# Mixer B's scan: the stabiliser rows arrive by broadcast transfers, and GpSimd makes the mask

## The chip, the cores and the metric

The kernel runs on one core of a Trainium2 chip. The metric is the device time of one execution in microseconds (us). A core has five engines that run on their own and meet at semaphores: TensorE (in the rows PE, its weight loads PEld), VectorE (DVE), ScalarE (ACT), GpSimd (POOL) and SyncE (SP), which here only issues transfers. 16 DMA engines move the data of all transfers.

## The reference

One step of a two-layer backbone with 128 context tokens ("prompt") and 1024 latent tokens, width 1024. Each layer computes modulation vectors from a conditioning vector, mixes tokens in three head groups (A: attention, B: a matrix memory scanned in both directions, C: neighbourhood attention), projects, and runs a channel MLP. The part that matters here is mixer B, 4 heads of 64, which the reference computes in chunks:

```python
def step(carry, xs):
    C, n, m = carry
    ...
    b = jnp.cumsum(fc, axis=1).transpose(0, 2, 1)
    d = jnp.where(causal, b[..., :, None] - b[..., None, :] + ig[..., None, :], -jnp.inf)
    inter = b + m[..., None]
    m_t = jnp.maximum(inter, jnp.max(d, axis=-1))
    w = jnp.einsum('blhd,bshd->bhls', qc, kc) * jnp.exp(d - m_t[..., None])
    w_inter = jnp.exp(inter - m_t)
    num = (jnp.einsum('bhls,bshd->blhd', w, vc)
           + jnp.einsum('bhl,blhk,bhkd->blhd', w_inter, qc, C))
    den = jnp.maximum(jnp.abs(den), jnp.exp(-m_t))
    ...

def modulation(cond, w_ada, b_ada):
    return jnp.split(jax.nn.silu(cond) @ w_ada + b_ada, N_MOD, axis=-1)
```

The running stabiliser m_t enters the weights of a chunk as a row: one value per head and query token, the same for all key tokens. Keys lie on the partitions, so this row has to be present on all 128 of them.

## The kernel before

Each layer runs its sections one after the other with a barrier between them: projection, mixer A, mixer C, mixer B, and the tail (output projection and MLP). The change lies in mixer B (`mixer_b`, lines 1734 to 1983), in what mixer C preloads for it, and in the constants.

**Items.** The scan has 18 items per layer: chunk of 128 tokens and direction, first the prompt's two, then the latent chunks, forward and backward in turn. Item i works on four heads at once. Every engine runs the items in order:

- TensorE, step i: scores(i+1) (line 1774, four products of 128x128, written to PSUM bank 0 or 1), spread(i+1) (line 1779), the product of queries and state (1793), the modulation pieces that belong to the step (430, 438, 447), W(i) (1798, weights times values), U(i) (1804, scaled keys times values).
- spread: four products of a constant selecting matrix `neg_select` with `m_rows`, where the stabiliser's rows of four heads lie on four partitions. The result, minus m_t on all partitions, is in bank 2.
- VectorE: weight(i) (1912, scores times E4), mask(i+1) (1905, spread plus the causal table, into E4), then finish(i-1): the N4 add (1919), four state updates (1926), the normalising steps (1930 to 1934), and for late items a sum of squares (1940).
- ScalarE: exp of E4 (1836), scaling of the state product (1843), and copies for the modulation.
- GpSimd, step i: KS(i), the scaling of the keys (1884), which U(i) needs. Once both directions of a chunk exist it also takes, at step i, the norm of item i-3 (1871, 1872, 1878) and the adding of the two directions of item i-2 (1860, 1864, 1866). Apart from the prompt's, these begin with step 12 (adding) and step 13 (norm), because the two directions meet in the middle.

E4, the exponents, has two buffers: mask(i) waits for weight(i-2).

**The modulation woven in.** The same loop multiplies the conditioning vector with 48 pieces of `w_ada` in layer 0 and 32 in layer 1, 512 KB each, 8 to a vector. They pass through a ring of 6 slots (`mods.w`, in `ring_flat`): piece c is loaded when piece c-6 has been used. Pieces 0 to 2 come from mixer C. Step 1 uses pieces 3 to 5, step 2 pieces 6 and 7, step 6 pieces 16 to 18, step 8 pieces 22 and 23, step 9 none (it turns a row into columns), step 10 pieces 24 to 27, step 11 pieces 28 to 31. SyncE issues all loads in one order; its waits are in that order too. After piece 5 it loads small rows (`load_rows`, which waits for `clear_rows` on GpSimd), and after pieces 17 and 25 it stores a gate row to DRAM, waits for the landing and broadcasts it back to all partitions (`spread_gate`, lines 487 and 491, two loads of 512 KB).

Of the kernel before, what the change touches and what calls it, by code (L numbers as in the profile page):

```python
# [19 lines left out]
ALU = mybir.AluOpType  # L20
# [5 lines left out]
P = 128  # L26
# [63 lines left out]
def shape_constants():  # L90
# [19 lines left out]
    neg_select = np.zeros((P, 2, 4, P), f)  # L110
# [4 lines left out]
    for j in range(4):  # L115
        for d in range(2):
            neg_select[32 * d + j, d, j] = -1
            for t in range(NT):
                r, c = 64 * d + 4 * t + j, LAT - 1 - t if d and t != PROMPT else t
                position[r, c] = 1  # L120
                gather[r, 32 * d + j] = 1
                spread[32 * d + j, r] = 1
                place[r, j, c] = 1
    bias_select = np.zeros((P, 4, 32), f)
    for j in range(4):
# [3 lines left out]
        "outside": np.where(neighbourhood_tables()[1], 0, NEG).astype(f), "neg_select": neg_select,  # L129
# [16 lines left out]
def build(nc, I, O):  # L146
    sems = {}
    with ExitStack() as ctx:
# [60 lines left out]
        neg_select = sb("neg_select_sb", [P, 2, 4, P])  # L209
# [32 lines left out]
        m_rows = rows_at_lo2[:, TABLE:TABLE + TOK]  # L242
# [73 lines left out]
        with nc.Block() as block:  # L316
            @block.sync
            def _(sp):
                for k, t in (("ident", ident[:, :]), ("causal", causal[:, :, :]), ("neg_select", neg_select[:, :, :, :]),
                             ("chunk_tables", chunk_tables[:, :]),  # L320
                             ("bias_select", bias_select[:, :, :])):
                    sp.dma_start(t, I[k]).then_inc(sem("constants_loaded"), 16)
                sp.wait_ge(sem("constants_loaded"), 5 * 16)
# [22 lines left out]
        for l in range(DEPTH):  # L346
# [18 lines left out]
            C_LOADS, C_TABLE_LOADS = 12 * 16, 2 * 16  # L365

# [1291 lines left out]
            def mixer_c():  # L1658
                with ExitStack() as own:
# [23 lines left out]
                    with nc.Block() as block:  # L1683
# [5 lines left out]
                        def _(pool):  # L1689
                            clear_low(pool, c_sets[1][2])  # L1690
                            pool.sem_inc(sem("c_low_cleared"), 1)
                            pool_step(pool.memset(m_rows, 0.0))
                            pool.sem_inc(sem("m_rows_cleared"), 1)
# [12 lines left out]
                        def _(sp):  # L1706
                            load_c(sp, 1, sem("c_loaded1"), sem("c_tables_loaded1"))
                            sp.wait_ge(sem("m_rows_cleared"), 1)
                            for d in range(2):
                                sp.dma_start(m_rows[32 * d:32 * d + 4, :].rearrange("h (t s) -> h t s", s=P),  # L1710
                                             stabiliser_dram[d].rearrange("t h s -> h t s")).then_inc(sem("b_loaded"), 16)
# [22 lines left out]
            def mixer_b():  # L1734
                with ExitStack() as own:
# [29 lines left out]
                    with nc.Block() as block:  # L1765
                        @block.tensor
                        def _(pe):
                            def scores(i):
                                d, t, c = work[i]
                                tt = slice(t * P, (t + 1) * P)  # L1770
                                if i >= 2:
                                    pe.wait_ge(sem("b_weighted"), i - 1)
                                for h in range(4):
                                    mm = pe.matmul(ps[:, i % 2, h * P:(h + 1) * P], kT[:, h // 2, h % 2, tt], qT[:, h // 2, tt], start=True, stop=True)
                                mm.then_inc(sem("b_scores"), 1)
                                if i >= 1:
                                    pe.wait_ge(sem("b_masked"), i)
                                for h in range(4):
                                    mm = pe.matmul(ps[:, 2, h * P:(h + 1) * P], neg_select[:, d, h, :], m_rows[:, tt], start=True, stop=True)
                                mm.then_inc(sem("b_stabiliser_spread"), 1)  # L1780
# [73 lines left out]
                        def _(pool):  # L1854
# [24 lines left out]

                            mods.clear_rows(pool)  # L1880
                            for i, (d, t, c) in enumerate(work):
                                if i >= 2:
                                    pool.wait_ge(sem("b_updated"), i - 1)
# [15 lines left out]
                        def _(dve):  # L1899
                            def mask(i):  # L1900
                                d, t, c = work[i]
                                dve.wait_ge(sem("b_stabiliser_spread"), i + 1)
                                if i >= 2:
                                    dve.wait_ge(sem("b_weighted"), i - 1)
                                dve.tensor_tensor(E4[:, i % 2, :].rearrange("p (h t) -> p h t", h=4), ps[:, 2, :].rearrange("p (h t) -> p h t", h=4),
                                                  causal[:, d:d + 1, :].to_broadcast([P, 4, P]), ALU.add).then_inc(sem("b_masked"), 1)

                            def weight(i):
                                dve.wait_ge(sem("b_exp"), i + 1)
                                if i >= 2:  # L1910
                                    dve.wait_ge(sem("b_applied"), i - 1)
# [30 lines left out]
                            mask(0)  # L1942
                            for i in range(nw):
                                weight(i)
                                if i + 1 < nw:
                                    mask(i + 1)
# [20 lines left out]
                        def _(sp):  # L1967
                            for c in range(3, mods.n * KD):
                                mods.load(sp, c)
                                if c == 5:  # L1970
                                    mods.load_rows(sp)
                                if c in (17, 25):
                                    mods.spread_gate(sp, mods.gates[c // 25])
# [522 lines left out]
```

## Time and profile before

| | us |
|---|---|
| median of 3 runs (lowest, highest) | 3462.75 (3461.22, 3467.98) |
| the profiled execution | 3457.57 |
| its span, first to last instruction | 3455.6 |
| TensorE busy in it | 3221.2 (93%) |
| VectorE, ScalarE, GpSimd busy | 1335.3, 1526.0, 1515.8 |
| share of the 16 DMA engines' time that the queues' packets took | 39.8% |
| mixer B's scan, layer 0 | 687.3 to 796 |
| mixer B's scan, layer 1 | 2392.2 to 2499 |

The span is what lies between the first and the last instruction; the execution's time has about 2 us around it. Times in the rows count from the span's start. A row of the timeline gives start and length of a run of equal instructions, with the idle time of the engine before it in square brackets and what ended that. A fp32 product of 128x128 shows as two instructions.

### The profile page before, as it was taken

How to read it: one execution, taken by the hardware profiler on the slowest of the kernel's cores; microseconds unless marked ns; L12 is line 12 of the kernel's file. 1: busy time of each engine (PE TensorE's matmuls, PEld its weight loads, DVE VectorE, ACT ScalarE, POOL GpSimd, SP SyncE). 2: the span in 40 equal slices, each digit the busy share in tenths (PEclk: the TensorE clock that was granted, in tenths of full speed). 3: DMA queues.
4: the chain of work that ended last, by engine and by line, in shares of the span. 5: the costliest groups of instructions: out<-in, count | busy, mean ns of one | idle time of the engine just before them, and what ended most of it. 6: DMA issues, size and time to landing. Idle time of an engine off the chain costs nothing. (4 is left out here: it accounts for less than half of the span.)

```text
span 3455.6 us, 50657 instructions
## 1 busy us (share of the span) xinstructions
PE 3221.2 (93%) x19786; PEld 2869.0 (83%) x19786; DVE 1335.3 (39%) x2283; ACT 1526.0 (44%) x2904; POOL 1515.8 (44%) x880
## 2 busy tenths in 40 slices
PE   4999899897899999999979998998789999999998
PEld 2999787785789889989869996887677899999897
DVE  3154366675621141141123435666756113112112
ACT  4223355544554454454442234554356444444443
POOL 1352101136655565565544321011467556556554
PEclk6999899998999999999989998999899999999999
DMA  5222401674544444444431223036355445444443
GB/s 202 55 81 99 127 1 43 176 278 135 174 130 125 145 134 126 143 133 124 145 101 41 85 102 110 1 90 200 131 175 160 127 125 162 128 124 153 139 123 115
DMA packets 357948, 429.43 MB, mean 124 GB/s; under 512 B 35328, under 2 KB 290320, under 8 KB 357200
## 3 DMA queue, kind: packets, MB, share of 16 engines
q1 hardware_dynamic: 357568, 426.07, 39.8%
q8 instruction: 159, 2.61, 0.3%
q14 instruction: 77, 0.63, 0.1%
q10 hardware_dynamic: 144, 0.13, 0.0%
HBM read 375.56 MB, written 50.57 MB: 123 GB/s over the span
## 5 line engine op out<-in xcount | busy, mean ns | idle before, releaser
L2330 POOL TENSOR_TENSOR w_lo<-w_raw,w_hi 128x1024 fp32r<-128x1024 f32 x432 | 1053.3, 2439 | 730.6 <-ACT w_hi L2251 730.5
L2251 ACT CAST w_hi<-w_raw 128x1024 fp32r<-128x1024 f32 x432 | 453.2, 1049 | 921.7 <-PE ps L2201 548.8
L2360 DVE TENSOR_TENSOR u_lo<-mix,u_hi 128x384 fp32r<-128x384 f32 x192 | 265.2, 1381 | 1208.0 <-ACT u_hi L2262 1208.0
L2199 PE MATMUL ps<-h_hi,w_hi 128*128 128x384 f32 x1536 | 519.8, 338 | 2.5 <-ACT mix L2258 2.5
L2201 PE MATMUL ps<-h_hi,w_lo 128*128 128x384 f32 x1536 | 519.1, 338 | 0.0
L2200 PE MATMUL ps<-h_lo,w_hi 128*128 128x384 f32 x1536 | 518.3, 337 | 0.0
L2216 PE MATMUL ps<-w_hi,u_hi 128*128 128x512 f32 x1152 | 456.1, 396 | 0.0
L2218 PE MATMUL ps<-w_hi,u_lo 128*128 128x512 f32 x1152 | 455.5, 395 | 0.0
L2217 PE MATMUL ps<-w_lo,u_hi 128*128 128x512 f32 x1152 | 454.6, 395 | 0.0
L1185 PE MATMUL ps<-h_hi,p_w_hi 128*128 128x384 f32 x960 | 331.0, 345 | 21.7 <-POOL p_w_lo L1399 21.7
L1187 PE MATMUL ps<-h_hi,p_w_lo 128*128 128x384 f32 x960 | 324.3, 338 | 0.0
L1186 PE MATMUL ps<-h_lo,p_w_hi 128*128 128x384 f32 x960 | 324.3, 338 | 0.0
L2199 PEld LDWEIGHTS ps<-h_hi,w_hi 128*128 128x128 f32 x1536 | 290.0, 189 | 11.0 <-issue 2.9
L2200 PEld LDWEIGHTS ps<-h_lo,w_hi 128*128 128x128 f32 x1536 | 290.0, 189 | 8.3
L2201 PEld LDWEIGHTS ps<-h_hi,w_lo 128*128 128x128 f32 x1536 | 289.9, 189 | 0.0
L2218 PEld LDWEIGHTS ps<-w_hi,u_lo 128*128 128x128 f32 x1152 | 216.3, 188 | 52.1
L2217 PEld LDWEIGHTS ps<-w_lo,u_hi 128*128 128x128 f32 x1152 | 216.6, 188 | 43.5
L2216 PEld LDWEIGHTS ps<-w_hi,u_hi 128*128 128x128 f32 x1152 | 216.7, 188 | 43.3
L1399 POOL TENSOR_TENSOR p_w_lo<-w_raw,p_w_hi 128x1024 fp32r<-128x1024 f32 x40 | 95.9, 2399 | 351.7 <-ACT p_w_hi L1294 351.7
L1185 PEld LDWEIGHTS ps<-h_hi,p_w_hi 128*128 128x128 f32 x960 | 181.9, 189 | 22.9 <-POOL p_w_lo L1399 22.5
L770 DVE TENSOR_REDUCE small<-ps 128x1 f32<-128x1152 f32 (+1 forms) x108 | 133.9, 1239 | 140.2 <-PE ps L688 139.9
L1186 PEld LDWEIGHTS ps<-h_lo,p_w_hi 128*128 128x128 f32 x960 | 182.0, 190 | 0.0
(267 smaller groups left out, 5294.8 us busy)
## 6 DMA issues: line engine op xcount, KB each, us to landing
w_raw<-in_w_ffn_up SPq DMA_DIRECT2D x192, 512.0 KB, 4.0
w_raw<-in_w_ffn_down SPq DMA_DIRECT2D x192, 512.0 KB, 3.3
ring<-in_w_ada SPq DMA_DIRECT2D x80, 512.0 KB, 5.9
w_raw<-in_w_in SPq DMA_DIRECT2D x34, 512.0 KB, 4.0
out_y_sample<-x SPq DMA_DIRECT2D x32, 512.0 KB, 3.0
w_raw<-in_w_out SPq DMA_DIRECT2D x30, 512.0 KB, 3.5
x<-out_y_sample SPq DMA_DIRECT2D x24, 512.0 KB, 4.9
w_raw<-in_w_out SPq DMA_DIRECT2D x36, 256.0 KB, 4.2
```

The source lines that it names most:

```text
L1185: pe.matmul(bank(q, CW), wh[:, k, :], hi[:, k, cc], start=(k == 0), stop=False)
L1186: pe.matmul(bank(q, CW), wh[:, k, :], lo(n)[:, k, :], start=False, stop=False)
L1187: mm = pe.matmul(bank(q, CW), wl[:, k, :], hi[:, k, cc], start=False, stop=(k == KD - 1))
L2199: pe.matmul(ps[:, 6, 0:CW], wh[:, k, :], hi[:, k, cc], start=(k == 0), stop=False)
L2200: pe.matmul(ps[:, 6, 0:CW], wh[:, k, :], lo(n)[:, k, :], start=False, stop=False)
L2201: mm = pe.matmul(ps[:, 6, 0:CW], wl[:, k, :], hi[:, k, cc], start=False, stop=(k == KD - 1))
L2216: pe.matmul(ps[:, b, :], a, w_hi[:, s % 3, cc], start=first, stop=False)
L2217: pe.matmul(ps[:, b, :], a, w_lo[:, s % 3, cc], start=False, stop=False)
L2218: mm = pe.matmul(ps[:, b, :], a_lo, w_hi[:, s % 3, cc], start=False, stop=end)
L2251: act.copy(w_hi[:, i % 3, :], raw[:, i % 3, :]).then_inc(sem("piece_hi"), 1)
L2330: pool.tensor_tensor(w_lo[:, i % 3, :], raw[:, i % 3, :], w_hi[:, i % 3, :].bitcast(F32), ALU.subtract).then_inc(sem("piece_lo"), 1)
L2360: dve.tensor_tensor(u_lo[:, j % 2, m, :], square[:, i % 2, :], u_hi[:, j % 2, m, :].bitcast(F32), ALU.subtract).then_inc(sem("m_u_lo"), 1)
```

## The change

The matmuls of the spread and the constant `neg_select` go. Instead the stabiliser rows of an item, 4 heads x 128 values = 2 KB in DRAM, are broadcast by one transfer to all 128 partitions (256 KB written), into one of five buffers. Rows of items 0 and 1 are loaded in mixer C, those of 2 to 4 at the start of the scan ahead of piece 3, that of item i+5 at SyncE's step i, after mask(i) is done. The mask moves from VectorE to GpSimd, is causal table minus row, and no longer reads PSUM. GpSimd makes mask(i+1) at the start of its step i, ahead of KS(i); masks 0 and 1 come ahead of `clear_rows`. weight(i) waits for scores(i) itself. SyncE now loads pieces by the step that frees their slot.

```diff
@@ shape_constants, build @@
-    neg_select = np.zeros((P, 2, 4, P), f)
...
-            neg_select[32 * d + j, d, j] = -1
...
-        m_rows = rows_at_lo2[:, TABLE:TABLE + TOK]
+        STABILISERS = 5
+        stabilisers = [rows_at_lo2[:, a:a + 4 * P] for a in (TABLE, TABLE + 512, TABLE + 1024, 0, 512)]
...
-                for k, t in (("ident", ident[:, :]), ("causal", causal[:, :, :]), ("neg_select", neg_select[:, :, :, :]),
+                for k, t in (("ident", ident[:, :]), ("causal", causal[:, :, :]), 
...
+            def load_stabilisers(sp, i, d, t, loaded):
+
+                row = stabiliser_dram[d, t:t + 1].rearrange("a h s -> a (h s)")
+                sp.dma_start(stabilisers[i % STABILISERS], row.to_broadcast([P, 4 * P])).then_inc(loaded, 16)
@@ mixer_c, GpSimd and SyncE @@
-                            pool_step(pool.memset(m_rows, 0.0))
-                            pool.sem_inc(sem("m_rows_cleared"), 1)
...
-                            sp.wait_ge(sem("m_rows_cleared"), 1)
                             for d in range(2):
-                                sp.dma_start(m_rows[32 * d:32 * d + 4, :].rearrange("h (t s) -> h t s", s=P),
-                                             stabiliser_dram[d].rearrange("t h s -> h t s")).then_inc(sem("b_loaded"), 16)
+                                load_stabilisers(sp, d, d, PROMPT, sem("b_loaded"))
@@ mixer_b, TensorE @@
-                                if i >= 1:
-                                    pe.wait_ge(sem("b_masked"), i)
-                                for h in range(4):
-                                    mm = pe.matmul(ps[:, 2, h * P:(h + 1) * P], neg_select[:, d, h, :], m_rows[:, tt], start=True, stop=True)
-                                mm.then_inc(sem("b_stabiliser_spread"), 1)
@@ mixer_b, GpSimd @@
+                            def mask(i):
+                                d, t, c = work[i]
+                                if i >= 2:
+                                    pool.wait_ge(sem(f"b_stabilisers_loaded{i % STABILISERS}"), 16 * ((i - 2) // STABILISERS + 1 if i % STABILISERS >= 2 else i // STABILISERS))
+                                    pool.wait_ge(sem("b_weighted"), i - 1)
+                                pool.tensor_tensor(E4[:, i % 2, :].rearrange("p (h t) -> p h t", h=4), causal[:, d:d + 1, :].to_broadcast([P, 4, P]),
+                                                   stabilisers[i % STABILISERS].rearrange("p (h t) -> p h t", h=4), ALU.subtract).then_inc(sem("b_masked"), 1)
+
+                            mask(0)
+                            mask(1)
                             mods.clear_rows(pool)
                             for i, (d, t, c) in enumerate(work):
+                                if 2 <= i + 1 < nw:
+                                    mask(i + 1)
@@ mixer_b, VectorE @@
-                            def mask(i):
...
                             def weight(i):
                                 dve.wait_ge(sem("b_exp"), i + 1)
+                                dve.wait_ge(sem("b_scores"), i + 1)
...
-                                if i + 1 < nw:
-                                    mask(i + 1)
@@ mixer_b, SyncE @@
-                            for c in range(3, mods.n * KD):
+                            def load_later(i):
+                                d, t, c = work[i]
+                                if i >= STABILISERS:
+                                    sp.wait_ge(sem("b_masked"), i - STABILISERS + 1)
+                                load_stabilisers(sp, i, d, t, sem(f"b_stabilisers_loaded{i % STABILISERS}"))
+
+                            step_of = {c: i for i in range(nw) for c in mod_pieces(i)}
+                            for i in range(2, STABILISERS):
+                                load_later(i)
+                            for c in range(3, mods.ring):
                                 mods.load(sp, c)
-                                if c == 5:
-                                    mods.load_rows(sp)
-                                if c in (17, 25):
-                                    mods.spread_gate(sp, mods.gates[c // 25])
+                            mods.load_rows(sp)
+                            for i in range(nw):
+                                if i + STABILISERS < nw:
+                                    load_later(i + STABILISERS)
+                                for c in range(mods.ring, mods.n * KD):
+                                    if step_of[c - mods.ring] == i:
+                                        mods.load(sp, c)
+                                        if c in (17, 25):
+                                            mods.spread_gate(sp, mods.gates[c // 25])
```

## Rows read from the trace of the kernel before

**Rows 1.** Timeline of layer 0's scan, TensorE in step 8: start, length, operation

```profile
733.09 0.97 PEld L1774 LDWEIGHTS ps<-hT 128*128 128x128 f32 x8
733.98 0.97 PEld L1779 LDWEIGHTS ps<-rows_at_lo,neg_select_sb 128*128 128x128 f32 x8
734.87 0.53 PEld L1793 LDWEIGHTS ps<-b_first,hT 128*128 128x128 f32 x4
...
736.95 0.97 PEld L1798 LDWEIGHTS ps<-b_first,b_weights 128*128 128x128 f32 x8 [0.41 <-issue]
...
738.29 0.97 PEld L1774 LDWEIGHTS ps<-hT 128*128 128x128 f32 x8
```

**Rows 2.** The same timeline, VectorE's weight(8)

```profile
733.37 0.69 DVE L1912 TENSOR_TENSOR b_weights<-ps,b_exponents 128x512 f32<-128x512 f32 x1 [0.21 <-DVE mix L1934]
```

**Rows 3.** SyncE's own waits, 686 to 790 us: total, times, longest

```profile
SPq L422 <- PE ps L430: 59.2, 20, 9.1
```

**Rows 4.** Windows: busy time by engine, granted clock, DMA share, GB/s

```profile
702.00:705.00 3.00, 3.00 (x36) 2.54 (x38) 1.86 (x5) 0.78 (x4) 0.00 (x0) 1.00 0.99 386
726.00:729.00 3.00, 3.00 (x31) 2.59 (x31) 2.29 (x8) 1.13 (x4) 0.61 (x1) 1.00 1.03 403
747.00:757.00 10.00, 10.00 (x112) 8.43 (x105) 5.72 (x18) 3.16 (x12) 3.29 (x5) 1.00 0.97 350
...
687.00:797.00 110.00, 96.90 (x1016) 81.06 (x1016) 77.73 (x215) 45.05 (x182) 44.91 (x68) 0.95 0.67 237
```

**Rows 5.** Timeline of GpSimd, steps 15 to 16 of layer 0

```profile
770.98 0.67 POOL L1884 TENSOR_TENSOR b_scaled_keys<-b_first,b_columns 128x256 f32<-128x256 f32 x1
771.83 0.19 POOL L1871 TENSOR_SCALAR small<-small 128x4 f32<-128x4 f32 x1 [0.18 <-DVE small L1940]
...
776.20 0.62 POOL L1884 TENSOR_TENSOR b_scaled_keys<-b_first,b_columns 128x256 f32<-128x256 f32 x1
```

**Rows 6.** Groups of GpSimd's instructions by shape, whole span: busy, mean ns

```profile
L1427 POOL TENSOR_TENSOR p_work<-mix,cos_sb 128x512 f32<-128x512 f32 x16 | 23.7, 1481 | 24.9 <-DVE mix L1458 24.9
L1433 POOL TENSOR_TENSOR p_work<-mix 128x512 f32<-128x512 f32 x18 | 21.2, 1182 | 0.0
```

**Rows 7.** Timeline of GpSimd at the scan's start

```profile
687.31 1.38 POOL L399 MEMSET mlp_mods_bias<- 128x1536 f32 x1 [24.52 <-remote]
```

**Rows 8.** Timeline of SyncE's issues in layer 0's scan

```profile
694.41 21.15 SPq L422 DMA_DIRECT2D ring<-in_w_ada  x12
715.60 1.19 SPq L487 DMA_DIRECT2D gate_rows<-mlp_mods_row  x4
718.94 0.82 SPq L491 DMA_DIRECT2D gate<-gate_rows  x2
```

**Rows 9.** Transfers issued 82 to 90 us: count, size, us to landing

```profile
cos_sb<-in_cos SPq DMA_DIRECT2D x1, 256.0 KB, 4.2
```

**Rows 10.** Windows, while the cosine table was in flight

```profile
85.50:86.00 0.50, 0.50 (x3) 0.50 (x3) 0.00 (x0) 0.47 (x1) 0.50 (x1) 0.50 1.18 403
```

**Rows 11.** Windows, while a gate row's two broadcasts were in flight

```profile
738.00:739.00 1.00, 1.00 (x11) 1.00 (x11) 0.68 (x2) 0.64 (x3) 0.36 (x1) 1.00 0.98 246
739.00:740.00 1.00, 1.00 (x12) 1.00 (x11) 0.36 (x1) 0.00 (x0) 0.26 (x1) 1.00 0.98 397
```

**Rows 12.** Timelines of VectorE: weight(12) and N4 of item 17, both layers

```profile
755.13 0.69 DVE L1912 TENSOR_TENSOR b_weights<-ps,b_exponents 128x512 f32<-128x512 f32 x1 [1.18 <-ACT b_exponents L1836]
...
787.34 0.43 DVE L1919 TENSOR_TENSOR b_intra<-ps,b_inter 128x260 f32<-128x260 f32 x1
...
2459.45 0.69 DVE L1912 TENSOR_TENSOR b_weights<-ps,b_exponents 128x512 f32<-128x512 f32 x1 [1.18 <-ACT b_exponents L1836]
...
2490.94 0.43 DVE L1919 TENSOR_TENSOR b_intra<-ps,b_inter 128x260 f32<-128x260 f32 x1
```

**Rows 13.** Timeline of SyncE at the start of the kernel

```profile
1.62 0.43 SPq L322 DMA_DIRECT2D neg_select_sb<-in_neg_select  x1
...
7.21 4.08 SPq L422 DMA_DIRECT2D w_ada_ring<-in_w_ada  x8
```

More of the change, by code:

```diff
@@ L128, in shape_constants @@
         "ident": ident, "cos": cos.copy(), "sin": sin.copy(), "causal": causal,
-        "outside": np.where(neighbourhood_tables()[1], 0, NEG).astype(f), "neg_select": neg_select,
+        "outside": np.where(neighbourhood_tables()[1], 0, NEG).astype(f),
         "chunk_tables": np.concatenate([position, gather, spread, place.reshape(P, 4 * NT)], 1), "bias_select": bias_select,
@@ L208, in build @@
         causal = sb("causal_sb", [P, 2, P])
-        neg_select = sb("neg_select_sb", [P, 2, 4, P])
         chunk_tables = sb("chunk_tables_sb", [P, NT + 36 + P + 4 * NT])
@@ L322, in _ @@
                     sp.dma_start(t, I[k]).then_inc(sem("constants_loaded"), 16)
-                sp.wait_ge(sem("constants_loaded"), 5 * 16)
+                sp.wait_ge(sem("constants_loaded"), 4 * 16)
             @block.gpsimd
@@ L1899, in _ @@
                         def _(dve):
-                            def mask(i):
[L1901 to L1906, printed above, removed]
                             def weight(i):
                                 dve.wait_ge(sem("b_exp"), i + 1)
+                                dve.wait_ge(sem("b_scores"), i + 1)
                                 if i >= 2:
@@ L1940, in sum_squares @@
                                 dve.tensor_reduce(ss[:, t, :], squares[:, n % 2, :].rearrange("p (h d) -> p h d", d=HD), AX.X, ALU.add).then_inc(sem("b_out_summed"), 1)
-                            mask(0)
                             for i in range(nw):
                                 weight(i)
-                                if i + 1 < nw:
-                                    mask(i + 1)
                                 if i >= 1:
```

## The prediction

> **What bounds the kernel now.** I read the page first: TensorE is busy 93% of the span, so time has to come off TensorE, or off a stretch where it waits. Then I read the stretch that the change touches, the scan of mixer B, which runs from 687.3 to 796 us in layer 0 and from 2392.2 to 2499 us in layer 1, on the timeline. One step of the loop is scores(i+1), spread(i+1), the state product, the weight pieces of the modulation, W(i) and U(i). In [rows 1] step 8 starts with its scores at 733.09 and step 9 at 738.29: 5.20 us, with TensorE's weight loads back to back but for 0.41 us, in which the 256-column products of the pieces still run. The spread takes 733.98 to 734.87, that is 0.89 us. VectorE in the same step [rows 2] starts weight(8) at 733.37, 3.6 us before W(8) needs it at 736.95: it isn't the bound. SyncE waits 59.2 us in all until TensorE has used a piece [rows 3]: the ring of pieces follows TensorE now. Reader, see here that TensorE bounds steps 1 to 11 and that the transfers are close behind: a window of 3 us reaches 403 GB/s at a share of 1.03 [rows 4].
>
> From step 13 on GpSimd is full. From one scaling of keys to the next it takes 5.22 us, of which 0.18 us is waiting [rows 5].
>
> **TensorE without the spread.** Steps 1 to 11 lose 11 x 0.89 = 9.8 us. In step 9 (no pieces) TensorE also waited about 0.8 us for VectorE's state update, which sat behind mask(10); with the mask off VectorE that goes too. At the start the first two spreads ran at the low clock; there I take 1.4 us. That is 12.0 us a layer, if nothing else is late. What is late next has to be looked for in the transfers and on GpSimd.
>
> **The transfers up to step 11.** SyncE's queue is in order. It gets three stabiliser loads ahead of pieces 3 to 5. Then it waits until GpSimd has cleared the modulation's rows. GpSimd now first makes mask(0) and mask(1). The nearest row is a 128x512 tensor_tensor with two tensors, one of them broadcast along the middle axis, at 1.48 us (one with a single input tensor took 1.18) [rows 6]; I take 1.48, because the mask also reads two tensors. So the clearing (1.38 us [rows 7] and a second memset of about 0.5) ends at about 692.4 instead of 689.3, and the small loads behind it, which ended just before 694.41 [rows 8], end at about 696.9. Piece 6 is issued there instead of at 694.41.
>
> From then on the queue never runs dry in my sum; this is its load until piece 31, the last one that step 11 needs:
> - pieces 6 to 31, 26 of 512 KB. At share 1 the windows give 386 to 403 GB/s [rows 4]; at 395 GB/s one takes 1.33 us: 34.6 us.
> - stabiliser rows 5 to 15, 11 of 256 KB in packets of 2 KB, none of which the scan has now. The nearest row by size is the cosine table, also 256 KB in rows of 2 KB [rows 9]; while it and its like were in flight the rate was 403 GB/s [rows 10]: 0.65 us. The nearest by kind is the gate row's broadcast, which started at 246 GB/s [rows 11]: 1.07 us, the upper bound. I take 0.70, since in the second half of the gate pair the rate was at 397: 7.7 us.
> - two pairs of gate broadcasts, 3.5 us each: 1.05 MB at about 300 GB/s, between the 246 and the 397 of [rows 11]: 7.0 us.
> - two bubbles. SyncE stores the gate row, waits for its landing and only then issues the broadcasts: 3.34 us from 715.60 to 718.94 [rows 8]. Now the stores stand behind a full queue, so the queue drains while SyncE waits; from landing to first data is 1.1 us, and landing trails the data by about 1.1: 2.2 us each, 4.4 us.
>
> Started at 699.2 (issue at 696.9 plus 2.3), the sum is 699.2 + 34.6 + 7.7 + 7.0 + 4.4 = 752.9. Landing, the last product, the bias, W(11) and U(11) add 3.2: step 12 starts at 756.1. Before it starts 0.38 us ahead of weight(12), which begins at 755.13 [rows 12]: 754.75. So the 12.0 us from the spreads are gone, and 1.3 us more. The reason in one line: three steps carry 8 pieces and now 3 stabiliser rows, 12.7 us of transfer in 12.9 us of shortened steps, and nothing is left for 11.4 us of gates and bubbles. In layer 1 the same sum starts 0.8 us earlier in the scan (fewer bias rows), against a step 12 that came at 66.9 us instead of 67.4: about +1.1 us.
>
> One page speaks on this rate: the Trainium skill, DMA: Bandwidth & Descriptors, section Specifications, puts HBM at about 358 GB/s for one core. The rows above show 386 and 403 GB/s here, so it isn't in the sum; by it a piece would take 1.46 us and each layer 3.4 us more.
>
> **GpSimd from step 12.** It gains one mask in each of steps 13 to 16. A step has 5.05 us of work ([rows 5], 5.22 less 0.18), with mask 1.55 (1.48 and a gap) 6.6 us. Followed step by step from step 12 (mask(14) after weight(12), then the keys, then the norm that waits for VectorE's sum, then the two directions), the last sum comes at 33.5 us and the N4 add of item 17 at 33.8 us after step 12's start. Before it came at 787.34 and 2490.94, weight(12) at 755.13 and 2459.45 [rows 12], so 32.6 and 31.9 us after step 12's start. That costs 1.2 us in layer 0 and 1.9 us in layer 1. With a mask of 1.20 it would cost 0.1 and 0.8. The wait that mask(i+1) adds, for weight(i-1) and for its row, holds the keys of item i behind it, and U(i) waits for those; a row lands 6 us or more ahead in my sum, so I put nothing there.
>
> **The rest.** neg_select (512 KB) leaves the constants, whose landing SyncE waited for: its issue at 1.62 and the first piece at 7.21 [rows 13]. Without it the constants land about 1.6 us earlier, and TensorE's wait for the first pieces moves with them: -1.6 us. In mixer C a memset and two small row loads go and two 256 KB loads come, 25 us before the next thing queued behind them: nothing. The added wait on scores in weight(i) is met: scores(i) ends a step ahead.
>
> **Sum:** -1.6 + (1.3 + 1.2) + (1.1 + 1.9) = +3.9 us. The profiled execution took 3457.57 us, with a span of 3455.6; that goes to 3461.5. The median of the three runs is 5.2 us above it; with the same step, 3462.75 + 3.9 = 3466.7.
>
> **The rivals.**
> - *The transfers stay hidden.* Then TensorE's 12.0 us stand in both layers, less 3.1 us for GpSimd's end, less 1.6: -22.5 us, 3440. For it: over 687 to 797 the queues were busy 0.67 of the time [rows 4], and SyncE mostly waited for TensorE. Against it: the sum above, which needs 11 us of slack by step 12 that I can't find.
> - *The broadcasts are slow (slower than before).* Sixteen queues read one 2 KB row. At 1.07 us a row each layer takes 11 x 0.37 = 4.1 us more: 3475. Were each to cost as long as a whole gate row at its slow start (2.1 us), it would be 15.4 us a layer: 3497. It decides from about 0.84 us a row on (11 x 0.14 = 1.5 us more a layer, which with the rest passes 3469.7). For it: the 246 GB/s. Against it: that may be a cold start, as the next row ran at 397.
> - *The rate sags under a constantly full queue.* From 747 to 757 it was 350 GB/s at a share of 0.97 [rows 4], 361 at a full one: 1.45 us a piece, 3.1 us more a layer, 3473. Against it: the higher rates stand beside it, and part of that window may be the drained end of a burst. The limit that the Trainium skill's page on DMA states would look like this.
> - *It doesn't do what it says in time:* SyncE is so late with rows that the masks come no earlier than before. The pace is then that of the transfers, as forecast; it gives about 3463.
>
> **Chances.** A measurement of this kernel can tell about 0.2% from no change, 6.9 us. The forecast has 0.50, of which 0.35 within 0.2%, 0.12 slower, 0.03 faster. Hidden transfers have 0.25, all faster, and here I count that they are only half hidden (3450). Slow broadcasts 0.15 and HBM 0.05 are slower. The last has 0.05: 0.03 same, 0.02 faster. Together: faster 0.30, same 0.38, slower 0.32. The forecast's own range is 3455 to 3476. The range for 8 in 10 reaches from 3443, which leaves out about half of the hidden case, to 3483, which leaves out the worst broadcasts.
>
> **What would show it.** No spread group and TensorE steps of 4.3 us early in the scan; then, from about step 6, TensorE idle ahead of the piece products with the ring's load as the releaser, 5 us at first and again at step 10 or 11; the transfer share near 1.0 from 700 to 750; the gate's stores waiting over 5 us; a GpSimd period of 6.6 us in steps 13 to 16; the first piece at 5.6 us. I am wrong if TensorE's step stays at 4.3 us up to step 11 (then 3440), or if stabiliser rows take over 1 us of all queues (then over 3475).

## The result, and the profile of the changed kernel

The changed kernel takes 3468.35 us (median of 22 runs, 3461.81 to 3474.44), the kernel before 3462.84 us on the same chips (22 runs). The ratio is 1.0018, with a 95% interval of 1.0011 to 1.0026: 5.5 us slower than before by the medians. That is under 0.2%, but the interval lies above 1. (One of the 22 runs of the kernel before took 6341 us; the ratio is of the fast runs alone.) The forecast was +3.9 us. The profiled execution of the changed kernel took 3471.58 us, its span is 3469.6 us; that is 14.0 us over the profiled span of before, so these two profiles lie further apart than the medians.

The measure I use for every kernel below is the length of a scan: from TensorE's first product of scores to the start of the N4 add of item 17. In the changed kernel it comes from these rows, the summary of the scores' products and of the N4 adds, layer 0 and then layer 1 (count, shortest, median and longest ns, first and last start).

```profile
L1773 PE MATMUL ps<-hT x144: 272/275/553, 682.7 to 773.4; 128*128 128x128 f32 x144
L1918 DVE TENSOR_TENSOR b_intra<-ps,b_inter x18: 418/419/430, 690.0 to 787.5; 128x260 f32<-128x260 f32 x18
L1773 PE MATMUL ps<-hT x144: 272/275/553, 2390.2 to 2485.5; 128*128 128x128 f32 x144
L1918 DVE TENSOR_TENSOR b_intra<-ps,b_inter x18: 419/419/430, 2397.2 to 2499.3; 128x260 f32<-128x260 f32 x18
```

That is 104.8 and 109.1 us. The same two groups of the kernel before give 99.9 and 98.7 us (its first scores stand at 687.4 and 2392.2, its last N4 adds in [rows 12]).

TensorE's weight loads on the timeline, steps 5 and 6 of layer 0 and the first loads of step 7, answer to [rows 1]:

```profile
711.15 0.97 PEld L1773 LDWEIGHTS ps<-hT 128*128 128x128 f32 x8
712.04 0.53 PEld L1787 LDWEIGHTS ps<-b_first,hT 128*128 128x128 f32 x4
...
715.47 0.97 PEld L1773 LDWEIGHTS ps<-hT 128*128 128x128 f32 x8
...
722.84 0.20 PEld L433 LDWEIGHTS ps<-ring,condT 128*32 128x32 f32 x8 [5.24 <-DMA ring<-in_w_ada]
723.85 1.78 PEld L1792 LDWEIGHTS ps<-b_first,b_weights 128*128 128x128 f32 x8 [0.81 <-issue]
725.51 0.98 PEld L1798 LDWEIGHTS ps<-b_first,b_scaled_keys 128*128 128x128 f32 x4
726.37 1.83 PEld L1773 LDWEIGHTS ps<-hT 128*128 128x128 f32 x8
```

The spread is gone and a step without a wait takes 4.32 us (711.15 to 715.47) instead of 5.20. In the next step TensorE stands for 5.24 us until piece 18 has landed. After that wait the same loads take 1.78 and 1.83 us where they took 0.97, because the clock has fallen. From the product that had waited to the next step's first product of a piece it is 5.95 us (722.84 to 728.79); two steps earlier the same stretch took 3.44 us (709.25 to 712.69). So the lower clock cost some 2.5 us there, besides the wait. The windows show both, with the columns of [rows 4]:

```profile
707.00:712.00 5.00, 4.44 (x50) 3.24 (x49) 4.54 (x14) 2.09 (x8) 4.45 (x7) 1.00 1.03 413
712.00:717.00 5.00, 5.00 (x55) 4.01 (x54) 2.69 (x10) 2.49 (x9) 2.28 (x3) 1.00 0.49 193
717.00:722.00 5.00, 1.08 (x17) 0.42 (x16) 3.26 (x9) 2.09 (x8) 3.23 (x4) 0.94 0.99 324
722.00:727.00 5.00, 4.16 (x22) 3.35 (x23) 0.60 (x2) 0.00 (x0) 0.21 (x2) 0.50 1.00 336
732.00:737.00 5.00, 5.00 (x57) 4.12 (x56) 3.16 (x11) 2.48 (x9) 1.70 (x2) 1.00 0.62 239
737.00:742.00 5.00, 4.53 (x47) 3.68 (x45) 4.46 (x15) 4.02 (x23) 2.87 (x3) 1.00 0.97 302
```

The reader should see three things. The transfer engines are idle half of 712 to 717 us and over a third of 732 to 737 (shares 0.49 and 0.62). After each gap they are busy again, but at 302 to 336 GB/s instead of 413. And the granted clock is at 0.50, the lower of TensorE's two levels (1.2 GHz), in the window behind the wait. The gaps fall where SyncE stands behind the gate's stores; these are its issues, to be set against [rows 8], and its own waits, against [rows 3]:

```profile
708.69 1.19 SPq L490 DMA_DIRECT2D gate_rows<-mlp_mods_row  x4
716.09 0.82 SPq L494 DMA_DIRECT2D gate<-gate_rows  x2
729.86 1.19 SPq L490 DMA_DIRECT2D gate_rows<-mlp_mods_row  x4
735.28 0.82 SPq L494 DMA_DIRECT2D gate<-gate_rows  x2
```

```profile
SPq L425 <- PE ps L433: 43.3, 20, 7.6
SPq L494 <- DMA gate_rows<-mlp_mods_row: 10.4, 2, 6.2
```

From stores to broadcasts it is now 7.4 and 5.4 us. In the kernel before it was 3.34 us the first time [rows 8] and 4.08 us the second (731.39 to 735.47).

### The profile page after: what moved, and what is told of

Read it like the earlier page. It is cut to its first block and busy times, and to the rows that moved or that the text cites. A ratio compares the mean times of both kernels' runs of the same rounds, so it can differ in the third digit from the quotient of the medians.

```text
span 3469.6 us, 50100 instructions
## 1 busy us (share of the span) xinstructions
PE 3206.6 (92%) x19498; PEld 2846.3 (82%) x19498; DVE 1310.4 (38%) x2247; ACT 1528.1 (44%) x2904; POOL 1558.0 (45%) x914
## 5 line engine op out<-in xcount | busy, mean ns | idle before, releaser
L1189 PEld LDWEIGHTS ps<-h_lo,p_w_hi 128*128 128x128 f32 x960 | 182.0, 190 | 0.0
```

What stands on the lines that cost most here:

```text
L1189: pe.matmul(bank(q, CW), wh[:, k, :], lo(n)[:, k, :], start=False, stop=False)
```

## The experiments

Each kernel was timed in five rounds beside the kernel before. The table gives the ratio to it with its 95% interval, and the two scans of the one profiled execution. A single scan scatters: the change, e8 and e11 have the same scan and give 104.8, 104.7 and 107.6 us in layer 0 and 109.1, 107.0 and 107.1 in layer 1. So a difference of 1 or 2 us between two scans says little.

| kernel | ratio to before | scans, layers 0 and 1 (us) |
|---|---|---|
| before | 1 | 99.9, 98.7 |
| the change | 1.0018 (1.0011 to 1.0026) | 104.8, 109.1 |
| e1 without rows 5 to 17 | 0.9971 (0.9960 to 0.9983) | 96.8, 96.8 |
| e2 masks on VectorE | 1.0026 (1.0015 to 1.0038) | 104.6, 106.7 |
| e3 gate broadcasts late | 0.9949 (0.9936 to 0.9963) | 91.1, 90.9 |
| e4 rows twice | 1.0109 (1.0093 to 1.0125) | 118.6, 116.1 |
| e5 = e2 and e3 | 0.9947 (0.9934 to 0.9959) | 91.8, 90.0 |
| e6 before, with e3's edit | 1.0003 (0.9995 to 1.0012) | 100.3, 98.6 |
| e7 broadcasts four pieces later | 0.9974 (0.9964 to 0.9985) | 95.9, 96.9 |
| e8 state stores late | 1.0020 (1.0011 to 1.0029) | 104.7, 107.0 |
| e9 = e3, last masks on VectorE | 0.9945 (0.9933 to 0.9957) | 90.4, 89.2 |
| e10 = e1 and e3 | 0.9935 (0.9923 to 0.9948) | 88.9, 89.5 |
| e11 a fifth constant | 1.0026 (1.0015 to 1.0037) | 107.6, 107.1 |
| e12 the wait alone | 0.9987 (0.9977 to 0.9997) | 104.1, 99.9 |

**e1: without the later stabiliser rows.** In SyncE's loop this goes, and the masks of items 5 to 17 wait for no row:

```diff
-                                if i + STABILISERS < nw:
-                                    load_later(i + STABILISERS)
```

> The kernel after the change, but the 13 stabiliser transfers of items 5 to 17 are left out in each layer (the mask of item i takes the row that lies in buffer i mod 5, so the output is not the reference's); all masks stay on GpSimd. Theory A (the change's gain on TensorE, 12 us per layer, is taken back by SyncE's queue of transfers): without 13 x 0.70 = 9.1 us of transfers per layer the waits for pieces at the scan's steps 6, 10 and 11 (5.2, 2.8 and 2.5 us in layer 0) shrink to under 2 us in all, and the time falls by 12 to 20 us, to 3448 to 3456. Rival B (GpSimd's masks take it back, by their 1.3 us in steps 13 to 16 and by the order of its work before): the piece waits shrink, but the time falls by less than 4 us. Rival C (the waits come from the gate's round trip, not from the rows): the wait at step 6 stays over 3 us and the time falls by 4 to 8 us.

The ratio falls from 1.0018 to 0.9971, 16 us, as theory A has it. TensorE's waits for pieces in layer 0 go from 16.1 to 8.9 us in all, not to under 2: something else in the queue is left. At step 6 it is still 3.54 us, the sign that rival C gave, though the time fell by far more than C's 4 to 8 us: rows and stops both carry it. GpSimd had the same masks to make, so rival B falls.

**e2: the masks on VectorE.** The tensor_tensor moves from GpSimd's loop to VectorE's:

```diff
@ GpSimd
-                                if 2 <= i + 1 < nw:
-                                    mask(i + 1)
@ VectorE
                                 weight(i)
+                                if i + 1 < nw:
+                                    mask(i + 1)
```

> The kernel after the change, but the mask is made by VectorE, one item ahead and in the place that it had before the change, from the stabiliser rows that the transfers brought: GpSimd is relieved of 18 x 1.3 = 23 us per layer, and the transfers stay. Theory A (transfers): the piece waits stay as they are (step 6 about 5 us), only the late steps 13 to 16 get back to a period of 5.2 instead of 6.3 us; that is 1 to 4 us per layer at most, time 3461 to 3467. Rival B (GpSimd): the time falls by 10 us or more, to under 3458.

1.0026, against 1.0018 for the change: no gain, and TensorE's waits for pieces stay (17.1 us in layer 0, against 16.1). By itself this would leave open that VectorE lost what GpSimd gained; with e1, where the masks stayed on GpSimd and the time fell, GpSimd is not what the change's gain was lost to.

**e3: the gate broadcasts behind the last piece.** The stores stay where they are (the second gate's wait until the first's have landed), and SyncE goes on to the next pieces:

```diff
-                    sp.wait_ge(self.sem("gate_stored"), 64 * (i + 1))
-                    for c in range(2):
-                        sp.dma_start(gate[:, s, c, :], ...)
@ after the last piece
+                            for v in mods.gates:
+                                mods.load_gate(sp, v)
```

> The kernel after the change, but SyncE issues the two pairs of gate broadcasts (4 x 512 KB) after the last piece instead of right behind the gate's stores, so that it waits for no store in the middle of its queue. Theory A: per layer two bubbles (the stores took 7.4 and 5.4 us to land, against a queue that drains in about 4 us) and 2 x 3.5 us of broadcasts go from before the last piece, some 7 to 11 us of the queue, of which the piece waits of step 6 (5.2 us) and of steps 10 and 11 (5.3 us in layer 0, more in layer 1) can give back 5 to 10 per layer: time 3449 to 3460. Rival C (the bubbles alone carry it, the rows nothing): the same or more, and then the run without rows gains under 8. Rival B (GpSimd): under 3 us gained.

It took 3438.14 us where the kernel before took 3457.72 on the same chip. The ratio of 0.9949 is 24 us under the change and 18 us under the kernel before; theory A had 8 to 19 us under the change. No wait for a piece is over 1.3 us any more. The change has a gain once the queue no longer stops.

**e4: each later row twice.** A second broadcast of the same row goes into a spare buffer.

```diff
+                                    sp.dma_start(spare[:, n % 2, :], row.to_broadcast([P, 4 * P])) ...
```

> The kernel after the change with a second transfer of each stabiliser row of items 5 to 17 into a spare buffer (13 x 256 KB more per layer, behind the first), which nobody reads. It measures the price of one row in the queue. Theory A (queue is the bound): 13 x 0.70 = 9.1 us per layer at the rate assumed in the prediction, 13 x 1.07 = 14 at the slower end; only the rows ahead of the last piece (11 to 12) count: +15 to +26 us in all, time 3484 to 3495. Rival B (the queue has slack in which a row is hidden): under +5 us.

31 us more than the change, over the upper end. The profile says why it can't be taken as the price of a row: the spare buffers are two, and SyncE stood for them itself, which it doesn't do in the change. This is its wait in layer 0:

```profile
SPq L1975 <- DMA spare_rows<-stabiliser_rows: 12.6, 4, 5.0
```

It shows once more that what is added to this queue is paid for. It doesn't tell what a row costs.

**e5: masks on VectorE, gate late.** The edits of e2 and e3 together.

> The kernel with the late gate broadcasts (e3: 0.9949 of the kernel before, scans of 91 us) and the masks on VectorE as in e2. Theory A2 (the queue's bubbles and the gate's 7 us set the end of the change's kernel; once they are gone, GpSimd is the bound of the late steps: busy without a gap from 750 to 776 us in e3, 6.4 us per step with a mask against 5.1 without): the scan gets shorter by 3 to 5 us per layer, ratio to before 0.992 to 0.9935. Rival B2 (VectorE pays for the mask what GpSimd saves, since each mask then stands in its chain between weight and the state's update): 0.9945 to 0.997, scans of 91 to 95 us.

0.9947 against 0.9949: neither side gains. The ratio is rival B2's.

**e6: the kernel before, with e3's edit alone.**

> The kernel before, with nothing changed but that the two pairs of gate broadcasts are issued after the last piece, as in e3. Theory A2: before the change TensorE set the pace of the scan (its waits for pieces were 1.3 us in layer 0), so the queue's bubbles were hidden: no change, 0.999 to 1.0005, so that of e3's gain 5 us over the kernel before need the change itself. Rival D (the gate's place is worth its 10 us per layer in either kernel and the change itself is worth nothing): 0.993 to 0.996.

1.0003, no change. So the late gates are worth nothing to the kernel before, where TensorE set the pace. The 18 us of e3 against before belong to both edits together: the change makes the transfers the bound, and the late gates make them short enough.

**e7: the broadcasts four pieces later.** This parts the standing still from the broadcasts' own time (spread_gate only stores here, as in e3).

```diff
                                         if c in (17, 25):
                                             mods.spread_gate(sp, mods.gates[c // 25])
+                                        if c in (21, 29):
+                                            mods.load_gate(sp, mods.gates[c // 29])
```

> The kernel after the change with the gate's stores where they are, and each pair of broadcasts four pieces later (behind pieces 21 and 29), so that SyncE doesn't stand still for the stores, but the 7 us of broadcasts stay ahead of the last pieces. It parts the bubble from the broadcasts' own time. If the bubble carries it (7.4 and 5.4 us from store to broadcast against a queue that drains in 4): most of e3's gain stays, 0.995 to 0.998 of before. If the broadcasts' 7 us per layer carry it: 0.999 to 1.001. Shares in proportion: 10 us per layer for both together in e3, of which bubbles 4.4 by the prediction's price would leave 0.998 to 0.999.

0.9974, over half of e3's gain. The windows of 40 us, from 712 to 752 us in layer 0, for the change, for e7 and for e12 (below):

```profile
712.00:752.00 40.00, 32.20 (x305) 24.98 (x304) 21.80 (x67) 14.76 (x62) 15.72 (x18) 0.87 0.89 314
```

```profile
712.00:752.00 40.00, 36.90 (x407) 29.07 (x405) 27.23 (x81) 21.95 (x91) 19.96 (x24) 1.00 1.00 391
```

```profile
712.00:752.00 40.00, 32.47 (x327) 23.59 (x326) 22.45 (x69) 14.71 (x62) 15.64 (x18) 0.93 0.87 301
```

With no stop, 391 GB/s for 40 us, pieces, rows and both pairs of broadcasts mixed, and the clock at its full level all the time. With the stops, 314 GB/s: 40 x (391 - 314) = 3.1 MB that did not come, 7.9 us at e7's rate. The shares, 1.00 and 0.89, tell how much of it is idle time: 4.4 us. The other 3.5 us are lost while the engines are busy; e12 shows on what.

**e8: the small stores of the states later.** `sp.wait_ge(sem("b_state_new"), 2)` becomes 13.

> The kernel after the change, but the 16 small stores of the states wait for item 12 instead of item 1, so that they are issued behind the landing of the last pieces. In the trace of the kernel after, layer 1's scan is 4.3 us longer than layer 0's (109.1 against 104.8) and its last pieces landed 12 us after their issue, with these stores behind them in the queue. If the stores slow the last pieces: layer 1's scan falls to about 105 and the time by 2 to 5 us (ratio to before 1.0005 to 1.001). If layer 1's excess is only the place where its waits fall, or a chance: no change, 1.0015 to 1.0025; if the stores end late: slower.

No change. The scan of layer 1 is longer than that of layer 0 in the changed kernel's profile for another reason, or by chance: in e11, which has the same scan, they are 107.6 and 107.1.

**e9: e3 with the last masks on VectorE.** `mask(i + 1)` is VectorE's from item 13 on.

> The kernel with the late gate broadcasts (e3), with the masks of items 13 to 17 alone on VectorE; items 0 to 12 stay on GpSimd. In e5, with all masks on VectorE, the last products of scores began 81 us into the scan against 77 in e3 (VectorE costs in the middle), but from there to the last sum it took 10.5 us against 14 (GpSimd costs at the end). Theory A2: the two add up, scans of 87 to 89 us against 91, 4 to 8 us off the whole, ratio to before 0.9925 to 0.994. Rival: GpSimd's backlog at step 12 is what the end waits for, and the last items gain nothing: 0.9945 to 0.9955, scans of 90 to 92.

0.9945, no gain over e3: the rival's outcome, though for another reason than it gave. In e3 GpSimd works without a gap at the scan's end, 6.42 us from one mask to the next; its timeline:

```profile
750.78 1.34 POOL L1884 TENSOR_TENSOR b_exponents<-causal_sb,rows_at_lo 128x512 f32<-128x512 f32 x1
752.08 0.61 POOL L1895 TENSOR_TENSOR b_scaled_keys<-b_first,b_columns 128x256 f32<-128x256 f32 x1
...
757.20 1.28 POOL L1884 TENSOR_TENSOR b_exponents<-causal_sb,rows_at_lo 128x512 f32<-128x512 f32 x1
```

In e9 VectorE is full instead, with 5.2 us to a step. Its timeline:

```profile
756.20 0.69 DVE L1924 TENSOR_TENSOR b_weights<-ps,b_exponents 128x512 f32<-128x512 f32 x1
756.81 0.68 DVE L1916 TENSOR_TENSOR b_exponents<-causal_sb,rows_at_lo 128x512 f32<-128x512 f32 x1
...
759.14 0.61 DVE L1943 TENSOR_TENSOR small<-small,b_columns 128x4 f32<-128x4 f32 x1
...
761.41 0.69 DVE L1924 TENSOR_TENSOR b_weights<-ps,b_exponents 128x512 f32<-128x512 f32 x1
...
774.44 0.16 DVE L1943 TENSOR_TENSOR small<-small,b_columns 128x4 f32<-128x4 f32 x1
```

The scans are 0.7 and 1.7 us shorter than e3's, and the time can't tell it.

**e10: e1 and e3 together.**

> Both reliefs at once: the gate broadcasts behind the last piece (e3) and no stabiliser transfers of items 5 to 17 (as in e1, so that masks of those items take other rows and the output is not the reference's). If e3 has brought the scan to the bound of TensorE and GpSimd, the rows are now hidden in the queue and leaving them out gives little: 0.9935 to 0.995 (e3 0.9949), scans of 89 to 91 us. If the queue is still the bound, the rows give their 8 us per layer again as in e1: under 0.991, scans of 84 to 86 us.

0.9935, with scans 2.2 and 1.4 us shorter than e3's; by the ratio it is 5 us for both layers, and the intervals overlap. So without the stops and the broadcasts ahead of the last pieces 13 rows per layer cost little, where with them (e1) they cost 8 and 12 us of scan.

**e11: a fifth constant.** Zeros of 512 KB in the place of neg_select.

> The kernel after the change with a fifth constant of 512 KB (zeros, in the place of neg_select) loaded among the others at the start. The prediction's term is 1.6 us for it: first piece issued 1.6 to 1.7 us later than in the kernel after (at 7.2 instead of 5.5 us) and the median 1 to 2 us up: ratio to before 1.0020 to 1.0025 (after: 1.0018). If the later stages swallow it (a transfer or an engine there that is late anyway): no change, and the first piece later all the same.

The first piece is issued at 7.38 us instead of 5.49, as expected. The time, 1.0026 against 1.0018, has the right sign, but the intervals overlap, so that the term is seen at the start and not proven in the sum.

**e12: the wait alone.** SyncE waits for the gate's stores as in the change, and the broadcasts come at the end:

```diff
                                             mods.spread_gate(sp, mods.gates[c // 25])
+                                            sp.wait_ge(mods.sem("gate_stored"), 64 * (c // 25 + 1))
```

> The fourth corner of a square: SyncE stands still at both gate stores until they have landed, as in the kernel after, but the broadcasts come behind the last piece, as in e3. The corners so far, as scans of layers 0 and 1: wait and broadcasts right behind it (the kernel after) 104.8 and 109.1 us, broadcasts alone (e7) 95.9 and 96.9, neither (e3) 91.1 and 90.9. In the trace of the kernel after the transfer engines stand idle for 2.5 and 1.9 us at the two waits, and then the rate stays at 184 to 377 GB/s in most windows of the next 4 and 8 us, with the broadcasts first in the empty queue, while in e7 the same broadcasts go at 390 to 430 in a full queue. Theory E (a broadcast that starts in an empty queue is what is slow, so wait and broadcasts cost more together than apart): the wait alone costs its idle 4.4 us per layer, scans of 94 to 97 us, ratio to before 0.996 to 0.998. Rival F (any restart of the queue is slow, or TensorE's clock falls behind the wait for a piece whatever stands first in it): scans of 99 to 104 us, ratio 0.998 to 1.001.

0.9987, scans of 104.1 and 99.9: F's numbers, not E's. Summed over both layers the corners are 182.0 us with neither, 192.8 with the broadcasts, 204.0 with the wait, 213.9 with both. By the scans the wait costs 22 us, the broadcasts 11, and together 32; by the ratios it is 13, 9 and 24 us. Either way they add up within the noise (layer by layer the scans do not: with the wait, the broadcasts cost 0.7 us in layer 0 and 9.2 in layer 1). Behind the first stop e12's queue has no gate broadcast in it, and yet its rate drops again 4 us after it has restarted. Windows of 1 us:

```profile
716.00:717.00 1.00, 1.00 (x11) 1.00 (x10) 0.39 (x1) 0.58 (x3) 1.00 (x2) 1.00 0.03 12
717.00:718.00 1.00, 1.00 (x12) 0.81 (x14) 0.99 (x4) 0.11 (x1) 1.00 (x3) 1.00 0.19 20
718.00:719.00 1.00, 0.85 (x16) 0.26 (x8) 0.94 (x4) 1.00 (x6) 1.00 (x2) 1.00 0.72 180
719.00:720.00 1.00, 0.00 (x0) 0.00 (x0) 0.93 (x3) 0.97 (x4) 0.82 (x2) 1.00 0.97 369
720.00:721.00 1.00, 0.21 (x4) 0.16 (x8) 0.72 (x3) 0.00 (x0) 0.00 (x0) 1.00 1.03 393
721.00:722.00 1.00, 1.00 (x14) 0.64 (x6) 0.45 (x1) 0.00 (x0) 0.41 (x1) 1.00 1.04 258
722.00:723.00 1.00, 1.00 (x9) 1.00 (x8) 0.08 (x1) 0.00 (x0) 0.86 (x1) 0.79 0.94 186
```

The first pieces are issued at 716.95; 20 and 180 GB/s are the time until their data run (shares 0.19 and 0.72), and then the pieces come at 369 and 393 GB/s. The two slow windows are where the first stabiliser row goes through, the third transfer in the queue: 2 KB packets, which only the rows have there, begin in them (82 and 35 of them), and in the second they take 248 ns in the median. In e7's full queue they take 84. So e12 doesn't have the wait alone: the rows are broadcasts too, and they stand behind the stop. e1 has stops and no later rows. These are its windows behind its first stop, the gate's broadcasts first, issued at 711.75, and then pieces alone:

```profile
713.00:714.00 1.00, 1.00 (x12) 1.00 (x11) 0.67 (x2) 0.30 (x2) 1.00 (x1) 1.00 0.93 250
714.00:715.00 1.00, 1.00 (x18) 0.71 (x20) 0.97 (x5) 0.40 (x2) 1.00 (x3) 1.00 0.99 229
715.00:716.00 1.00, 0.57 (x12) 0.08 (x4) 0.95 (x3) 1.00 (x6) 1.00 (x2) 1.00 0.99 406
716.00:717.00 1.00, 0.00 (x0) 0.00 (x0) 0.90 (x3) 0.69 (x3) 0.55 (x1) 1.00 1.01 410
```

From 715 to 724 it stays at 397 to 426 GB/s. Behind e1's second stop the broadcasts are at 274 and 217 GB/s again, and the pieces then at 311 to 397 for five windows. So what is slowest behind a stop is a broadcast, of a gate or of a row; the pieces are slowed less, and behind the first stop not at all. That leans to theory E's mechanism, though its number for e12 was missed, and no run has the wait with neither rows nor broadcasts behind it. Why a broadcast is slow there and not in a full queue stays open.

## Why the prediction was right, and where it wasn't

**The mechanism was right.** TensorE loses 0.88 us a step, the queue of transfers takes it back, and the waits fall where they were forecast: 5.24 us in step 6 (forecast: about 5), then 2.8 us in step 10 and 2.5 in step 11 (forecast: 5 again). Steps 1 to 4 wait another 5.5 us in all, which the forecast did not place. e1 and e3 show the mechanism by relieving the queue, e2 and e5 by leaving GpSimd's masks out of it. Rival "the transfers stay hidden" is what e3 is: 0.9949 is 3445 us on the scale of 3462.8, between the 3440 and the 3450 given for it.

**The bubbles were mis-sized.** The term was 2 x 2.2 = 4.4 us a layer. The idle time itself was that: shares of 0.49 and 0.62 in two windows of 5 us leave 2.5 + 1.9 = 4.4 us. But it stands for more than idle time. The change's queue fell 7.9 us behind e7's in layer 0, 4.4 us of it idle and 3.5 us in broadcasts that ran slowly behind the stops and what ran beside them, and the lower clock behind the long wait came on top. e12 against e3 puts the wait at 13.0 and 9.0 us of scan, and in time at 0.0038 of 3463, 13 us for both layers, against 8.8 in the sum. This is the term that was mis-sized most.

**The other terms of the queue.** The gate pairs were put at 7.0 us a layer; e7 against e3 gives 4.8 and 6.0 us of scan. The 11 rows were put at 7.7; leaving 13 rows out (e1 against the change) gives 8.0 and 12.3, with the stops. The rows' own price can be read from the changed kernel's trace: a row is 8 packets of 2 KB for each of the 16 engines, and a packet took 108 ns in the mean in layer 0 and 106 in layer 1, so a row took 0.86 and 0.85 us of all engines where the sum had 0.70. That is some 1.7 us more a layer. The rival of slow broadcasts is therefore half true: it was to decide from 0.84 us on and the rows are just beyond that, and a broadcast behind a stop is slow, but the mean stays well under its 1.07 us. In e7's full queue, from 712 to 752, a packet took 86 ns, 0.69 us a row. The rival of a sagging rate, and the 358 GB/s that the prediction quoted from the Trainium skill, DMA: Bandwidth & Descriptors, fall with e7's 391 GB/s. The Trainium skill's page Perfetto Trace Analysis, section Roofline, says that the 358 GB/s is the share when both cores of a pair draw on the memory, and that one core alone may pass it up to about 435 GB/s; 391 here over 40 us agrees.

**The start of the queue** was right: piece 6 was forecast 9.6 us after the scan's start (696.9 against 687.3) and issued at 692.28, 9.6 us after 682.7.

**GpSimd's end.** The period was forecast at 6.6 us, with a mask at 1.48. The masks took 1.29 us in the mean, and from one scaling of keys to the next it was 6.35 and 6.30:

```profile
765.04 0.61 POOL L1890 TENSOR_TENSOR b_scaled_keys<-b_first,b_columns 128x256 f32<-128x256 f32 x1
771.39 0.62 POOL L1890 TENSOR_TENSOR b_scaled_keys<-b_first,b_columns 128x256 f32<-128x256 f32 x1
777.69 0.61 POOL L1890 TENSOR_TENSOR b_scaled_keys<-b_first,b_columns 128x256 f32<-128x256 f32 x1
```

From weight(12) to the last N4 add it took these distances, against [rows 12]:

```profile
755.10 0.69 DVE L1911 TENSOR_TENSOR b_weights<-ps,b_exponents 128x512 f32<-128x512 f32 x1 [5.83 <-ACT b_exponents L1830]
...
787.47 0.43 DVE L1918 TENSOR_TENSOR b_intra<-ps,b_inter 128x260 f32<-128x260 f32 x1
...
2465.51 0.69 DVE L1911 TENSOR_TENSOR b_weights<-ps,b_exponents 128x512 f32<-128x512 f32 x1 [10.10 <-ACT b_exponents L1830]
...
2499.34 0.43 DVE L1918 TENSOR_TENSOR b_intra<-ps,b_inter 128x260 f32<-128x260 f32 x1
```

That is 32.4 and 33.8 us, where it was 32.2 and 31.5: +0.2 and +2.3, against +1.2 and +1.9 in the sum. The loss lies ahead of step 12: weight(12) comes 72.4 and 75.3 us after the scan's first product, and it was 67.7 and 67.3. So +4.7 and +8.1 us, where the sum had +1.3 and +1.1.

**Why the total came out so near all the same.** The two scans grew by 4.9 and 10.4 us in the profiles, not by 5.5 us together. What the profiles leave outside of the scans shrank: it is 3255.7, 3253.0 and 3250.0 us in the three profiles with the change's scan (the change, e8, and e11 with its fifth constant), and 3257.0 and 3259.2 in the two with the scan of before (before, e6). The mean difference is 5 us. The forecast had -1.6 us there, for the constants, but e11, which has that constant's transfer back, has the smallest value of the three, so the constants do not explain it. Nor is it firm: over all twelve changed kernels the rest goes from 3249.8 to 3258.7 us. I can't place it: the windows in which the granted clock falls are others in each execution, outside the scan too. The medians, +5.5, lie below what the mean of these profiles would give (about +10). So the mechanism was foreseen, but that the total came so near is luck: the scans were forecast to grow by 5.5 us together and grew by 13 to 16 in the three profiles, and what lies between that and +5.5 is a shrinkage elsewhere of about 5 us, which no run explains, and another 4 us or so between these profiles and the medians.

## What to carry to other kernels

When an edit relieves the bounding engine beside a busy in-order transfer queue, first look in that queue for an issuer that waits for a landing (a store that is read back): what was 3.3 and 4.1 us in a queue with slack becomes 7.4 and 5.4 behind a full one, and its price is above its idle time (8.8 us idle in two layers; 13 us by the ratio, 22 by the scans), with the broadcasts that run slowly behind it and the clock behind the wait. Issue the store, go on with the loads, and fetch it back behind the last one that is urgent; that edit alone gave nothing to the kernel before (e6), and together with the change 0.5% against it (e3). A new bound can hide two edits from each other: try them together, too.

## What the runs showed of the hardware that I had not expected

- A broadcast that goes through soon after the queue has stood still is slow, and a plain piece much less so: 184 to 250 GB/s for the gate's broadcasts at the first stop (the change and e1), 186 and 258 around e12's first row, against 397 to 426 for the pieces behind e1's first stop (311 to 397 behind its second) and 391 over 40 us with everything mixed in e7. A packet of a row took 84 ns in the full queue and 248 in the median in e12's slowest window.
- Behind a wait of 5.24 us for a transfer TensorE's granted clock was 0.50 for 5 us, and eight weight loads took 1.78 instead of 0.97 us. In e7, whose waits for a piece are 2.0 us at most, every window from 712 to 752 had 1.00. The length of one wait does not decide it alone: in the changed kernel it also fell to 0.50 at 745 us, behind two waits of 1.72 and 1.12 us with a short product between them.
- On VectorE a 128x4 tensor_tensor took 0.61 us where it usually takes 0.16 (the rows of e9), while GpSimd was at work. The Trainium skill, SBUF — State Buffer, section SBUF: two separate sides, has a rule for this, that VectorE with two inputs in SBUF and GpSimd hold a shared pair of ports one after the other for a whole instruction. The rows agree: VectorE's operation ran from 759.14 to 759.75, and GpSimd's instruction beside it in e9's timeline ends at 759.73:

```profile
759.12 0.61 POOL L1863 TENSOR_TENSOR b_squares<-mix 128x256 f32<-128x256 f32 x1
```
